# Rotary embedding of the first block: the exchanged halves come by SBUF transfers in place of a TensorE permutation matmul

## The chip, the cores and the metric
One NeuronCore of one Trainium2 chip runs the whole program. The metric is the device time of one execution in microseconds (us). The times of three executions of the kernel before stand below. All readings of a trace are of one profiled execution.

## What is computed
Two blocks, each with two layers, run over one sequence of 256 tokens with 1024 channels, in float32. Only the first block's projection and its rotary embedding matter here (cut from the reference):

```
def apply_rope(x, positions):
    half = HEAD_DIM // 2                     # HEAD_DIM = 64
    ...
    x1, x2 = xf[..., :half], xf[..., half:]
    return jnp.concatenate([x1 * cos - x2 * sin, x2 * cos + x1 * sin], axis=-1)

h = rms_norm(x, attn_pre_gain)
u = h @ w_in
(qa, ka, va, qb, kcb, vcb, ksb, vsb, kwb, vwb, g_nsa, g_a, g_b) = split(u)
qa, ka, qb_rot, ks, kw = apply_rope of qa, ka, qb, ksb, kwb
```

Attention over a window, over compressed and over selected keys follows, then an output projection, and a feed-forward network with a convolution. The second block has no rotary embedding.

## The kernel before
**Layout.** The projection `u` is held transposed: 128 channels (two heads of 64) on the partitions and 256 tokens along each. One such [128, 256] array is a tile of `U1`. In each of the two layers (`L`) of the first block there are 16 tiles, numbered t = 0 to 15. Eleven of them are rotated: `ROPE = [0, 1, 2, 3, 4, 6, 7, 8, 9, 12, 14]`, and their place in this list is r. Tiles 5, 13 and 15 are values (`VALS`), which are transposed; 10 and 11 are inputs of the compression.

**Weights.** Weights stream from HBM in chunks of about 1 MB, in a fixed order c0, c1, ... that is counted anew for each layer here: c0 to c7 are the eight panels of `w_in`, and panel x gives the tiles 2x and 2x+1. Then come c8 (branch gates), c9 (first compression weight), c10 (gates), c11 (second compression weight), c12 and c13 (gates), c14 (branch output). SyncE (SP) issues two transfers of 512 KB for each into one of three slots of `raw`; the load of chunk n waits until chunk n-3 has been split (`wlo_ready`, `load`). ScalarE (ACT) rounds a chunk to `whi` (L543), VectorE (DVE) subtracts to get `wlo` (L891): the two halves that give a float32 product out of rounded ones. Both run in a ring of four.

**A tile.** TensorE (PE) multiplies `whi` and `wlo` with the activations (L1452, L1455) into one of four banks of PSUM. ACT copies the low part out (`low`), DVE adds it (L899) into `U1`, which counts up `tile_out`. PE waits at tile t for the sum of tile t-4.

**The rotation of a tile (before).** PE multiplies the tile in float32 with `C("swap")`, a 128x128 permutation that exchanges partitions i and i^32 within each 64 (L1650), into bank 6 or 7. GpSimd (POOL) writes `cq` = tile x cos (L1355). DVE writes `tm` = bank x signed sin (L1038) and adds `cq` to it (L1041), in place in `U1` or, for tiles 6 to 9, into `QR`. `tm` and `cq` have two buffers each.

**Order.** Each engine runs its own list in program order. DVE's step c (0 to 11, the loop over `in_cs`) is: split a chunk (c+3), sum the tiles 2c and 2c+1, then `rope(r)` for the rotated ones among the tiles 2c-2 and 2c-1. In layer 0, while c is under 4, the split stands at the end of the step. In layer 0, step 2 also has `parameters()`, and step 3 the split of the gate weights. Steps 6 and 7 end with `cmp_build`, and steps 7 and 8 have `cmp_lo`, which feeds the compression. ACT's step c is: round chunk c+3, copy low parts, and, after a key tile (4, 12, 14), wait for its rotation and copy it with exchanged heads (`KSW`). PE's step c is: the two tiles of panel c, then the matmuls with `swap` of tiles 2c-2 and 2c-1, and the transposes of a value tile (L1662), which wait for its sum and, for tile 5 in layer 0, for `params_ready`. At c = 4 PE multiplies gate weights (L1627), at c = 5 it does four small products (L1633, L1634). At c = 8 the first gates' tiles are interleaved with the first compression (L1601), which waits for the sum of tile 14 and for `cmp_lo(0)`.

**SP's list.** For each layer it is c0, c1, ..., c6, then the two gain vectors broadcast into `G1` and `G2` (`gains`, L447 and L441, 512 KB written by each), then c7, c8 and so on.

Of the kernel before, what the change touches and what calls it, by code (L numbers as in the profile page):

```python
# [10 lines left out]
ALU = mybir.AluOpType  # L11
# [5 lines left out]
S = 256  # L17
# [22 lines left out]
Z_MAX = 20.0  # L40


CONST = {"ident": 128, "swap": 128, "ntri": 128, "stick": 128, "mask_a": 256, "mask_c": 256, "pair": 24,
         "mask_cmp": 32, "count": 32, "width": 2, "freq": 1, "sign": 1}
CONST_AT, _n = {}, 0
for _k, _w in CONST.items():
# [5 lines left out]
def host_constants():  # L52

    c = np.zeros((P, CONST_COLS), np.float32)

    def put(name, a):
        at, w = CONST_AT[name]
        c[:, at:at + w] = np.asarray(a, np.float32).reshape(P, w)
    i = np.arange(P)
    put("ident", np.eye(P))  # L60
    put("swap", (i[:, None] == (i ^ 32)[None, :]))
    put("ntri", np.where(i[:, None] >= i[None, :], -1.0, 0.0))
    put("stick", np.where(i[:, None] < i[None, :], 0.0, NEG))
    tri = np.where(i[None, :] <= i[:, None], 0.0, NEG)
    put("mask_a", np.concatenate([np.where(i[None, :] > i[:, None], 0.0, NEG), tri], 1))
    put("mask_c", np.concatenate([np.zeros((P, P)), tri], 1))
    put("pair", (i[:, None] % 24 == np.arange(24)[None, :]) & (i[:, None] < 48))
    end = np.arange(16) * 16 + 31
    end[15] = 1 << 20
    t = np.stack([i, i + P], 1)  # L70
    put("mask_cmp", np.where(end[None, None, :] <= t[:, :, None], 0.0, NEG))
    width = np.where(i[:, None] < 64, [[2, 8]], [[4, 16]])
    put("count", 1.0 / np.minimum(np.arange(1, 17)[None, None, :], width[:, :, None]))
    put("width", 1.0 / width)
    put("freq", np.float32(10000.0) ** (-(i % 32).astype(np.float32) / np.float32(32)))
    put("sign", np.where(i % 64 < 32, -1.0, 1.0))
    return c
# [90 lines left out]
def build(nc, a, out):  # L168
# [120 lines left out]
    wg_hi, wg_split, gates_part, gates_copied = sem("wg_hi"), sem("wg_split"), sem("gates_part"), sem("gates_copied")  # L289
    cur_ready, gain_ready = sem("cur_ready"), sem("gain_ready")  # L290
    gates_sum, gates_ready = sem("gates_sum"), sem("gates_ready")
    swap_ready, swap_used = sem("swap_ready"), sem("swap_used")
    cosmul_ready, rope_done, kswap_done = sem("cosmul_ready"), sem("rope_done"), sem("kswap_done")
    vt_ready, vt_out = sem("vt_ready"), sem("vt_out")
    cmp_in, cmp_hi, cmp_rhs, cmp_hid = sem("cmp_in"), sem("cmp_hi"), sem("cmp_rhs"), sem("cmp_hid")
# [128 lines left out]
    def _(sp):  # L424
# [26 lines left out]
        def panel(c, w_, c0):  # L451
# [2 lines left out]
            d = raw[:, c % RAW, :].rearrange("p (k n) -> p k n", n=256)  # L454
            load(c, [(d[:, x:x + 4], v[:, x:x + 4]) for x in (0, 4)])

        def two(c, views):

            d = raw[:, c % RAW, :].rearrange("p (m k n) -> p m k n", m=2, n=P)
            load(c, [(d[:, m], v_.rearrange("(k p) n -> p k n", p=P)) for m, v_ in enumerate(views)])  # L460
# [17 lines left out]
        sp.dma_start(const[:, 0:P], a["const"][:, 0:P]).then_inc(ident_in, 16)  # L478
        for L, p in enumerate(PLAN.one):
            n = 2 * L  # L480
            for s, (c, _) in enumerate(p["in"]):
                panel(c, a["w_in"][L], s * 256)
                if c == 0:
                    sp.dma_start(X[:, 1, :], a["x"][0, P:2 * P, :]).then_inc(x_in[1], 16)
                    sp.dma_start(posi[:, :], a["positions"][0:1, :].broadcast_to([P, S])).then_inc(consts_in, 16)
                    sp.dma_start(const[:, at:], a["const"][:, at:]).then_inc(consts_in, 16)
                if c == 1:
                    sp.dma_start(const[:, P:at], a["const"][:, P:at]).then_inc(masks_in, 16)
                if s == 6:
                    gains(n + 1)  # L490
            for j in range(EARLY):
                gate(L, j, p["early"][j][0])
                if j < 2:
                    c = p["cmp"][j][0]
                    v = a["cmp_w1"][L, j].rearrange("(k p) n -> p k n", p=P)
                    d = raw[:, c % RAW, :].rearrange("p (k n) -> p k n", n=P)
                    load(c, [(d[:, x:x + 8], v[:, x:x + 8]) for x in (0, 8)])
            for kind, x, c, _ in p["branch"]:
                if kind == "gate":
                    gate(L, x, c)  # L500
                else:
                    d = raw[:, c % RAW, :].rearrange("p (b k n) -> p b k n", b=2, n=256)
                    load(c, [(d[:, b], a[nm][L, :, x * 256:x * 256 + 256].rearrange("(k p) n -> p k n", p=P))
                             for b, nm in enumerate(("w_branch_a", "w_branch_b"))])
            token_major(p["out"], a["w_out"][L])
            for j, (c, _) in enumerate(p["up"]):
                two(c, [a["ffn_w_up"][L, :, j * P + b * FF:j * P + b * FF + P] for b in range(2)])
                if j == 6:
                    gains(n + 2)
            token_major(p["down"], a["ffn_w_down"][L])  # L510
# [368 lines left out]
    def _(dve):  # L879
# [149 lines left out]
        for L, p in enumerate(PLAN.one):  # L1029
# [3 lines left out]
            def rope(r):  # L1033

                t = ROPE[r]
                dst = U1[:, PLACE[t], :] if t < 6 or t > 9 else QR[:, t - 6, :]
                dve.wait_ge(swap_ready, 11 * L + r + 1)
                v.tensor_tensor(tm[:, r % 2, :], bank[6 + r % 2][:, 0:S], sinT[:, :], ALU.mult).then_inc(swap_used, 1)  # L1038
                dve.wait_ge(swap_used, 11 * L + r + 1)
                dve.wait_ge(cosmul_ready, 11 * L + r + 1)  # L1040
                v.tensor_tensor(dst, cq[:, r % 2, :], tm[:, r % 2, :], ALU.add).then_inc(rope_done, 1)  # L1041

            def cmp_build(n):

# [390 lines left out]
    def _(pe):  # L1435
# [150 lines left out]
        for L, p in enumerate(PLAN.one):  # L1586
# [28 lines left out]
            for c in range(9):  # L1615
# [26 lines left out]
                                                  rows[:, r, :], ident)  # L1642
                    ins.then_inc(rows_t, 1)
                for t in (2 * c - 2, 2 * c - 1):
                    if t in ROPE:
                        r = ROPE.index(t)
                        pe.wait_ge(tile_out, t0 + t + 1)
                        if r >= 2:
                            pe.wait_ge(swap_used, 11 * L + r - 1)
                        mm(bank[6 + r % 2][:, 0:S], C("swap"), U1[:, PLACE[t], :], start=True, stop=True, **g32)\  # L1650
                            .then_inc(swap_ready, 1)
                    if t in VALS:
                        n = VALS.index(t)
                        pe.wait_ge(tile_out, t0 + t + 1)
                        if n:
                            pe.wait_ge(vt_out, 3 * L + n)
                        elif L == 0:
                            pe.wait_ge(params_ready, 1)
                        else:
                            pe.wait_ge(tile_out, t0 + 6)  # L1660
                        for b in range(2):
                            ins = nc.tensor.transpose(bank[5][:, b * P:b * P + P], U1[:, PLACE[t], b * P:b * P + P], ident)  # L1662
                        ins.then_inc(vt_ready, 1)
# [3 lines left out]
            pe.wait_ge(cmp_hid, 2 * L + 2)  # L1667
            pe.wait_ge(vt_out, 3 * L + 3)
            pe.wait_ge(cur_ready, L + 1)
            pe.wait_ge(swap_used, 11 * L + len(ROPE))  # L1670
            mm(bank[6][:, 0:30], w2cur[:, :, :].rearrange("p r d -> p (r d)"), HC[:, 0, :], start=True, stop=True, **g32)
            for g in range(2):
                ins = mm(bank[6][0:N_CMP, P + HD * g:P + HD * g + HD], HC[:, 1, N_CMP * g:N_CMP * g + N_CMP], w2all[:, L, 1, :],
# [236 lines left out]
```

## Time and profile before

| | us |
|---|---|
| three executions | 1738.45, 1739.1 and 1739.48; median 1739.1 |
| the profiled execution, first to last instruction (its span) | 1735.3 |
| TensorE busy | 1704.5 (98%) |
| VectorE busy | 1216.0 (70%) |
| ScalarE busy | 1021.0 (59%) |
| GpSimd busy | 691.9 (40%) |
| bytes moved by the transfers | 306.73 MB, mean 177 GB/s |

The executions are 3.8 us longer than the span of the profiled one: that is what lies before the first and after the last instruction. Shares are averages over stages with different limits. The stage of the change lies at 28 to 82 us in layer 0 and at 419 to 468 us in layer 1. The granted clock of TensorE is at its full level in all slices of the page.

### The profile page before, as it was taken

The page shows a single profiled execution, that of the slowest core. Times are in us where ns is not written, and L with a number is a line of the kernel's source. Part 1 is how long each engine was busy: PE and PEld are TensorE (multiplying, and loading weights), DVE is VectorE, ACT ScalarE, POOL GpSimd, SP SyncE. Part 2 cuts the span into 40 slices and gives each one's busy share as a digit, 9 for nine tenths or more (in the row PEclk, how much of TensorE's full clock was granted, in tenths as well). Part 3 has the DMA queues.
Part 4 walks back from the last instruction along what each step waited for, and adds up shares of the span by engine and source line. Part 5 has one row for each costly group of instructions (what it writes and reads, how often), then busy time and mean ns, then how long its engine had stood idle before and what let it go on. Part 6 is the DMA issues. An engine that isn't in the chain of part 4 may idle for free.

```text
span 1735.3 us, 26430 instructions
## 1 busy us (share of the span) xinstructions
PE 1704.5 (98%) x9926; PEld 1453.6 (84%) x9926; DVE 1216.0 (70%) x1840; ACT 1021.0 (59%) x1928; POOL 691.9 (40%) x666
## 2 busy tenths in 40 slices
PE   8999999999999999999999999999999999999998
PEld 6867898888867888889888887888898889788887
DVE  7776799967766799957666656766476656566663
ACT  5587666655577666646555556555465545565542
POOL 4134346601034256604661050775057600507640
PEclk9999999999999999999999999999999999999999
DMA  9633666576524567576766553866576565348662
GB/s 267 179 98 113 175 197 177 177 241 175 148 80 122 170 197 192 179 234 172 193 182 222 181 168 98 232 185 204 180 202 187 182 230 194 122 123 223 188 208 73
DMA packets 412226, 306.73 MB, mean 177 GB/s; under 512 B 10083, under 2 KB 366901, under 8 KB 412098
## 3 DMA queue, kind: packets, MB, share of 16 engines
q1 hardware_dynamic: 411314, 304.31, 59.8%
q8 instruction: 79, 1.29, 0.3%
q0 software_dynamic: 784, 0.72, 0.2%
q14 instruction: 49, 0.40, 0.1%
HBM read 303.94 MB, written 1.05 MB: 176 GB/s over the span
## 4 chain that ended last, share of the span: by engine, by line
PE 76%; DVE 15%; ACT 4%; issue 3%; DMA 2%; SPq 0%; DVEq 0%; ACTq 0%
PE bank L1452 24%; PE bank L1455 12%; PE bank L1550 8%; PE bank L1552 8%; PE bank L1551 8%; DVE wlo L891 6%; DVE CB L1216 6%; PE bank L1503 3%; PE bank L1516 3%; PE bank L1513 3%; DVE UB L899 2%; DMA raw<-in_w_in 2%; ACT whi L543 1%; PE bank L1757 1%; ACT PB L546 1%
## 5 line engine op out<-in xcount | busy, mean ns | idle before, releaser
L891 DVE TENSOR_TENSOR wlo<-raw,whi 128x1024 fp32r<-128x1024 f32 (+1 forms) x568 | 734.8, 1319 | 176.2 <-ACT whi L543 172.8
L1452 PE MATMUL bank<-hsA,whi 128*128 128x512 f32 x2480 | 796.6, 398 | 0.6 <-DVE TA L899 0.6
L543 ACT ACTIVATE whi<-raw 128x1024 fp32r<-128x1024 f32 (+1 forms) x568 | 571.4, 1034 | 136.3 <-PE bank L1552 88.7
L1455 PEld LDWEIGHTS bank<-hsA,wlo 128*128 128x128 f32 x2480 | 466.2, 188 | 105.4
L1455 PE MATMUL bank<-hsA,wlo 128*128 128x256 f32 x2480 | 495.0, 279 | 0.0
L1452 PEld LDWEIGHTS bank<-hsA,whi 128*128 128x128 f32 x2480 | 384.1, 189 | 4.1 <-issue 3.3
L543 ACT ACTIVATE low<-bank 128x256 f32<-128x256 f32 (+1 forms) x404 | 150.2, 376 | 314.3 <-PE bank L1452 283.5
L1320 POOL TENSOR_TENSOR HB<-CB,UB 128x256 f32<-128x256 f32 x88 | 123.6, 1405 | 344.5 <-ACT CB L546 343.9
L1550 PE MATMUL bank<-whi,hid 128*128 128x512 f32 x528 | 206.1, 390 | 2.0 <-DVE wlo L891 2.0
L1552 PE MATMUL bank<-wlo,hid 128*128 128x512 f32 x528 | 205.5, 389 | 0.0
L1551 PE MATMUL bank<-whi,hid 128*128 128x512 f32 x528 | 205.4, 389 | 0.0
L899 DVE TENSOR_TENSOR UB<-bank,low 128x256 f32<-128x256 f32 x264 | 109.2, 416 | 114.9 <-ACT low L543 114.7
L1321 POOL TENSOR_TENSOR hid<-CB,UB 128x256 fp32r<-128x256 f32 x88 | 144.8, 1646 | 0.0
L1550 PEld LDWEIGHTS bank<-whi,hid 128*128 128x128 f32 x528 | 99.1, 188 | 22.9 <-DVE wlo L891 2.8
L1320 POOL TENSOR_TENSOR HB<-CB 128x256 f32<-128x256 f32 x44 | 61.9, 1408 | 140.6 <-ACT CB L546 140.6
L1552 PEld LDWEIGHTS bank<-wlo,hid 128*128 128x128 f32 x528 | 99.1, 188 | 20.6
L1551 PEld LDWEIGHTS bank<-whi,hid 128*128 128x128 f32 x528 | 99.1, 188 | 20.5
L1216 DVE SCALAR_TENSOR_TENSOR CB<-UB,convT,CB 128x256 f32<-128x256 f32 x176 | 114.0, 705 | 0.0
L1322 POOL TENSOR_TENSOR hid<-HB,hid 128x256 fp32r<-128x256 f32 x132 | 109.7, 831 | 10.4
L1516 PE MATMUL bank<-hsA,wlo 128*128 128x256 f32 x464 | 96.5, 284 | 3.1 <-ACT hsA L543 3.1
L1513 PE MATMUL bank<-hsA,whi 128*128 128x256 f32 x464 | 94.2, 283 | 0.0
L1516 PEld LDWEIGHTS bank<-hsA,wlo 128*128 128x128 f32 x464 | 78.8, 192 | 5.0 <-issue 5.0
(226 smaller groups left out, 1885.5 us busy)
## 6 DMA issues: line engine op xcount, KB each, us to landing
raw<-in_ffn_w_up SPq DMA_DIRECT2D x176, 512.0 KB, 5.2
raw<-in_ffn_w_down SPq DMA_DIRECT2D x120, 512.0 KB, 4.6
raw<-in_w_in SPq DMA_DIRECT2D x104, 512.0 KB, 5.9
raw<-in_ffn_w_gate SPq DMA_DIRECT2D x88, 512.0 KB, 4.0
raw<-in_w_out SPq DMA_DIRECT2D x32, 512.0 KB, 4.5
raw<-in_ffn_w_down SPq DMA_DIRECT2D x24, 256.0 KB, 3.0
G<-in_norm_g SPq DMA_DIRECT2D x12, 512.0 KB, 7.1
raw<-in_cmp_w SPq DMA_DIRECT2D x8, 512.0 KB, 5.0
```

Of the source, the lines that this page charges most:

```text
L543: return nc.scalar.activation(out_, in_, func, **kw)
L891: v.tensor_tensor(wlo[c_ % RING][:, x:y], raw[:, c_ % RAW, x:y], whi[c_ % RING][:, x:y].bitcast(F32), ALU.subtract)\
L1216: ins = v.scalar_tensor_tensor(y[:, n, :], UB[:, j % 2, n, k:S + k], convT[:, k, at:at + 1], y[:, n, :], ALU.mult, ALU.add)
L1320: g_.tensor_tensor(HB[:, j % 2, :], x, y, ALU.mult)
L1321: seq.link(g_.tensor_tensor(dst[:, 0:S], x, y, ALU.mult))
L1452: return mm(out_[:, 0:2 * n], whi[slot][:, at:at + P], rhs[:, 0:2 * n], start=x == 0, stop=False, **g32)
L1455: return mm(out_[:, n:2 * n], wlo[slot][:, at:at + P], rhs[:, 0:n], start=False, stop=False, **g32)
L1513: return mm(out_, whi[c % RING][:, at(m, k):at(m, k) + P], both(k, 1), start=False, stop=j == 0 and k == KD - 1, **g32)
L1516: return mm(tile_bank(t + m)[:, S:2 * S], wlo[c % RING][:, at(m, k):at(m, k) + P], hsA[:, k, 0:S], start=False, stop=j > 0 and k == KD - 1 ...
L1550: mm(y, hi, whi[s][:, x * HALF:x * HALF + HALF], start=k == k_first, stop=False, **g32)
L1551: mm(y, lo, whi[s][:, x * HALF:x * HALF + HALF], start=False, stop=False, **g32)
L1552: ins = mm(y, hi, wlo[s][:, x * HALF:x * HALF + HALF], start=False, stop=k == k_end, **g32)
```

## The change
The matmul with `swap` is gone, with its constant, its PSUM banks and PE's waits. SP now issues four transfers from SBUF to SBUF for each rotated tile. Each copies 32 partitions of the tile (32 KB) to the partitions of the other half, in the `tm` buffer of the tile. DVE multiplies that buffer in place with the signed sine. Before each group of four, SP waits for the tile's sum and for the end of the rotation two places before, which frees the buffer. The groups of panel x stand in SP's list right before the load of chunk x+7, in layer 0 for x under 4 right before that of chunk x+6. The constants are 128 columns narrower.

```
-                dve.wait_ge(swap_ready, 11 * L + r + 1)
-                v.tensor_tensor(tm[:, r % 2, :], bank[6 + r % 2][:, 0:S], sinT[:, :], ALU.mult).then_inc(swap_used, 1)
+                q = 11 * L + r
+                turned = tm[:, q % 2, :]
+                dve.wait_ge(swap_ready[q % 2], 64 * (q // 2) + 64)
+                v.tensor_tensor(turned, turned, sinT[:, :], ALU.mult).then_inc(swap_used, 1)
...
-                        pe.wait_ge(tile_out, t0 + t + 1)
-                        if r >= 2:
-                            pe.wait_ge(swap_used, 11 * L + r - 1)
-                        mm(bank[6 + r % 2][:, 0:S], C("swap"), U1[:, PLACE[t], :], start=True, stop=True, **g32)\
-                            .then_inc(swap_ready, 1)
...
+        def swap_rows(L, x):
+            for t in (2 * x, 2 * x + 1):
+                if t in ROPE:
+                    r = ROPE.index(t)
+                    q = 11 * L + r
+                    sp.wait_ge(tile_out, PLAN.one[L]["in"][0][1] + t + 1)
+                    if r >= 2:
+                        sp.wait_ge(rope_done, q - 1)
+                    for b in range(4):
+                        sp.dma_start(tm[32 * b:32 * b + 32, q % 2, :], U1[32 * (b ^ 1):32 * (b ^ 1) + 32, PLACE[t], :])\
+                            .then_inc(swap_ready[q % 2], 16)
...
+            behind = {first + x + (6 if L == 0 and x < 4 else 7): x for x in range(8)}
+            def turns_before(c):
+                if c in behind:
+                    swap_rows(L, behind[c])
             for s, (c, _) in enumerate(p["in"]):
+                turns_before(c)
                 panel(c, a["w_in"][L], s * 256)
```

`turns_before(c)` stands in the same way before the loads of the gates, of the compression weights and of the branch output.

## Rows read from the trace of the kernel before

**Rows 1.** The page: span, busy time of each engine, and the chain that ended last.
```profile
span 1735.3 us, 26430 instructions
...
PE 1704.5 (98%) x9926; PEld 1453.6 (84%) x9926; DVE 1216.0 (70%) x1840; ACT 1021.0 (59%) x1928; POOL 691.9 (40%) x666
...
PE 76%; DVE 15%; ACT 4%; issue 3%; DMA 2%; SPq 0%; DVEq 0%; ACTq 0%
```
**Rows 2.** Busy time by stretch: length, then PE, PEld, DVE, ACT, POOL, clock, DMA share, GB/s.
```profile
28.00:71.00 43.00, 42.80 (x243) 36.40 (x242) 38.10 (x65) 23.09 (x39) 13.48 (x17) 1.00 0.86 237
...
420.00:457.00 37.00, 36.50 (x202) 30.26 (x200) 30.04 (x51) 17.87 (x32) 7.68 (x9) 1.00 0.73 205
```
**Rows 3.** The instructions of L1650: duration min/median/max in ns, first and last start.
```profile
L1650 PE MATMUL bank<-U,const x44: 377/379/483, 28.0 to 466.1; 128*128 128x256 f32 x44
```
**Rows 4.** The chain in order of time, PE's part of L1650: start, us.
```profile
49.74 0.86 PE bank L1650 x4
```
**Rows 5.** TensorE in order of time: start, us, line, operation, [idle before].
```profile
41.94 0.38 PE L1662 MATMUL bank<-const,U 128*128 128x128 f32 x2
...
70.91 0.27 PE L1601 MATMUL bank<-RH,whi 128*128 128x60 f32 x1 [0.20 <-DVE U L899]
...
419.44 1.02 PE L1650 MATMUL bank<-U,const 128*128 128x256 f32 x4
420.64 1.46 PE L1650 MATMUL bank<-U,const 128*128 128x256 f32 x4 [0.18 <-DVE tm L1038]
427.53 0.59 PE L1650 MATMUL bank<-U,const 128*128 128x256 f32 x2
...
456.93 0.27 PE L1601 MATMUL bank<-RH,whi 128*128 128x60 f32 x1 [0.20 <-DVE U L899]
```
**Rows 6.** VectorE in order of time, layer 0.
```profile
31.24 0.41 DVE L1038 TENSOR_TENSOR tm<-bank,sinT 128x256 f32<-128x256 f32 x1
...
34.50 2.89 DVE L891 TENSOR_TENSOR wlo<-raw,whi 128x1024 fp32r<-128x1024 f32 x2
...
39.66 0.43 DVE L1041 TENSOR_TENSOR U<-cq,tm 128x256 f32<-128x256 f32 x1
...
64.60 0.42 DVE L899 TENSOR_TENSOR U<-bank,low 128x256 f32<-128x256 f32 x1 [2.14 <-ACT low L543]
```
**Rows 7.** VectorE in order of time, layer 1.
```profile
420.07 0.42 DVE L1038 TENSOR_TENSOR tm<-bank,sinT 128x256 f32<-128x256 f32 x1 [1.93 <-PE bank L1650]
...
433.53 2.36 DVE L891 TENSOR_TENSOR wlo<-raw,whi 128x1024 fp32r<-128x1024 f32 x2 [2.26 <-ACT whi L543]
```
**Rows 8.** ScalarE in order of time, layer 1: the key tile, then the next chunk.
```profile
431.31 0.84 ACT L543 ACTIVATE KSW<-U 64x256 f32<-64x256 f32 x2 [3.19 <-DVE U L1041]
```
**Rows 9.** Issues at 28 to 29 us: name, queue, count, KB, us from issue to landing.
```profile
raw<-in_w_in SPq DMA_DIRECT2D x1, 512.0 KB, 9.8
```
**Rows 10.** The same, issues at 414.6 to 415.2, then at 417 to 418 us.
```profile
G<-in_attn_post_gain SPq DMA_DIRECT2D x1, 512.0 KB, 9.4
...
raw<-in_w_in SPq DMA_DIRECT2D x1, 512.0 KB, 8.7
```
**Rows 11.** The same, small issues at 0 to 20 us.
```profile
const<-in_const SPq DMA_DIRECT2D x1, 34.0 KB, 8.0
...
rows<-in_pool_scale POOLq DMA_DIRECT2D x1, 2.0 KB, 2.1
```
**Rows 12.** SP's queue in order of time: start, us for the issue, line.
```profile
1.19 0.32 SPq L477 DMA_DIRECT2D gain<-in_attn_pre_gain  x1
...
4.01 0.87 SPq L486 DMA_DIRECT2D const<-in_const  x1
...
28.01 0.76 SPq L435 DMA_DIRECT2D raw<-in_w_in  x1
...
415.43 1.16 SPq L441 DMA_DIRECT2D G<-in_ffn_pre_gain  x1
...
76.83 0.37 SPq L435 DMA_DIRECT2D raw<-in_w_branch_a  x1
```

More of the change, by code:

```diff
@@ L40 @@
 Z_MAX = 20.0
-CONST = {"ident": 128, "swap": 128, "ntri": 128, "stick": 128, "mask_a": 256, "mask_c": 256, "pair": 24,
+CONST = {"ident": 128, "ntri": 128, "stick": 128, "mask_a": 256, "mask_c": 256, "pair": 24,
          "mask_cmp": 32, "count": 32, "width": 2, "freq": 1, "sign": 1}
@@ L60, in host_constants @@
     put("ident", np.eye(P))
-    put("swap", (i[:, None] == (i ^ 32)[None, :]))
     put("ntri", np.where(i[:, None] >= i[None, :], -1.0, 0.0))
@@ L291, in build @@
     gates_sum, gates_ready = sem("gates_sum"), sem("gates_ready")
-    swap_ready, swap_used = sem("swap_ready"), sem("swap_used")
+    swap_ready, swap_used = [sem("swap_ready0"), sem("swap_ready1")], sem("swap_used")
     cosmul_ready, rope_done, kswap_done = sem("cosmul_ready"), sem("rope_done"), sem("kswap_done")
@@ L480, in _ @@
             n = 2 * L
+            first = p["in"][0][0]
+            behind = {first + x + (6 if L == 0 and x < 4 else 7): x for x in range(8)}
+            def turns_before(c):
+                if c in behind:
+                    swap_rows(L, behind[c])
             for s, (c, _) in enumerate(p["in"]):
+                turns_before(c)
                 panel(c, a["w_in"][L], s * 256)
@@ L491, in _ @@
             for j in range(EARLY):
+                turns_before(p["early"][j][0])
                 gate(L, j, p["early"][j][0])
@@ L494, in _ @@
                     c = p["cmp"][j][0]
+                    turns_before(c)
                     v = a["cmp_w1"][L, j].rearrange("(k p) n -> p k n", p=P)
@@ L498, in _ @@
             for kind, x, c, _ in p["branch"]:
+                turns_before(c)
                 if kind == "gate":
@@ L1036, in rope @@
                 dst = U1[:, PLACE[t], :] if t < 6 or t > 9 else QR[:, t - 6, :]
-                dve.wait_ge(swap_ready, 11 * L + r + 1)
-                v.tensor_tensor(tm[:, r % 2, :], bank[6 + r % 2][:, 0:S], sinT[:, :], ALU.mult).then_inc(swap_used, 1)
+                q = 11 * L + r
+                turned = tm[:, q % 2, :]
+                dve.wait_ge(swap_ready[q % 2], 64 * (q // 2) + 64)
+                v.tensor_tensor(turned, turned, sinT[:, :], ALU.mult).then_inc(swap_used, 1)
                 dve.wait_ge(swap_used, 11 * L + r + 1)
                 dve.wait_ge(cosmul_ready, 11 * L + r + 1)
-                v.tensor_tensor(dst, cq[:, r % 2, :], tm[:, r % 2, :], ALU.add).then_inc(rope_done, 1)
+                v.tensor_tensor(dst, cq[:, r % 2, :], turned, ALU.add).then_inc(rope_done, 1)
             def cmp_build(n):
@@ L1644, in _ @@
                 for t in (2 * c - 2, 2 * c - 1):
-                    if t in ROPE:
-                        r = ROPE.index(t)
-                        pe.wait_ge(tile_out, t0 + t + 1)
-                        if r >= 2:
-                            pe.wait_ge(swap_used, 11 * L + r - 1)
-                        mm(bank[6 + r % 2][:, 0:S], C("swap"), U1[:, PLACE[t], :], start=True, stop=True, **g32)\
-                            .then_inc(swap_ready, 1)
                     if t in VALS:
@@ L1669, in _ @@
             pe.wait_ge(cur_ready, L + 1)
-            pe.wait_ge(swap_used, 11 * L + len(ROPE))
             mm(bank[6][:, 0:30], w2cur[:, :, :].rearrange("p r d -> p (r d)"), HC[:, 0, :], start=True, stop=True, **g32)
```

## The prediction

> **What bounds the kernel now.** I read the page first: TensorE is busy for 98% of the span and carries 76% of the chain that ended last [rows 1]. Taken alone that says that every matmul removed is time won. But shares are averages, so the next view is the busy time of the stretch in which the rotations lie. In layer 0, from 28 to 71 us, PE is busy for 42.80 of 43 us, and DVE for 38.10: DVE has only 4.9 us to spare in seven and a half steps. In layer 1, from 420 to 457, DVE has 37 - 30.04 = 7.0 us to spare [rows 2]. So PE binds, and DVE is close behind it, closest in layer 0. The same rows show the transfers at a share of 0.86 and 0.73.
>
> PE in order of time shows where the two meet: the first compression matmul, at 70.91 and at 456.93, waits for a DVE sum [rows 5]. Before it stands DVE's wait of 2.14 us for tile 13 at 64.60 [rows 6], then `cmp_build`, a split, `cmp_lo` and the sum of tile 14, some 6.3 us of DVE work without a gap. I call this point the meeting. Whatever moves the meeting moves everything behind it, and I work out its shift for each layer.
>
> **What is removed.** A rotated tile has two instructions on L1650, 44 in all for 22 tiles [rows 3]. Their 379 ns overlap; what they occupy is read from the chain: four take 0.86 us, so 0.43 us a tile [rows 4]. Nine tiles lie ahead of PE's last tiles before the meeting: 3.9 us in layer 0. In layer 1 the first four tiles cost more, since PE waits there for `tm` to free a bank: from 419.44 to about 421.8, 2.3 us (the second four start at 420.64 and end with a stall on their buffers) [rows 5]; with five more (2.2 us) 4.5 us. The eleventh tile comes behind the meeting, 0.43 us. If nothing else happened and DVE kept up, 22 x 0.43 = 9.5 us, and some more in layer 1, would be the gain.
>
> **What is added on DVE.** The multiplication reads `tm` and not PSUM. The two DVE operations of a rotation, one of which reads PSUM and one only SBUF, take 0.41 and 0.43 us where nothing disturbs them [rows 6], so I count no difference. Removing DVE's wait for PE (1.93 us in layer 1 [rows 7]) is worth something only if the rows are there sooner than the matmul was.
>
> **What is added on SP and the transfers.** There are 88 transfers of 32 KB. No row shows one from SBUF to SBUF. Two prices are needed.
> - *Issue.* The nearest rows are 0.32 us (4 KB) and 0.37 us (512 KB, quiet queue); while the queue is full the 34 KB constant took 0.87 and a gain 1.16 [rows 12]. I take 0.4 us, that of the quiet rows with a gap, so 1.6 us a tile and 3.2 us for a panel of two. The ends are 0.32 and 0.87.
> - *Landing.* The floor is the 2.1 us of a 2 KB transfer on a quiet queue. A small transfer behind loads lands late: the 34 KB constant took 8.0 us [rows 11]. I take it that a transfer lands no sooner than the load issued before it on SP's queue, and at least 2.1 us after its issue.
>
> The Trainium skill, in "DMA: Bandwidth & Descriptors", under "Anatomy of one DMA", gives a transfer a fixed cost of about 2.0 us and little more at this size; by that alone the rows would always be in time, and the sum would be that of rival B. The same page, under "Queues, rings and completion order", has each DMA engine consume descriptors in ring order, which speaks against this change: the rows stand behind whatever SP issued before. The constant's 8.0 us is on the side of the second, and no row shows a small SBUF transfer overtaking a load.
>
> **Layer 0, step by step.** SP's groups for panel 0 stand behind c5. The second half of c5 is issued at 28.01, taking 0.76, and lands 9.8 us later, at 37.8 [rows 9, 12]. The rows of tiles 0 and 1 are issued by 32.0 but land at about 38. DVE wanted them at 31.24 [rows 6]: it now stands still for nearly 7 us. Queued behind that wait on DVE are the rotations, the split of c4, the sums of tiles 4 and 5, and `parameters`. From 38.2: two rotations (1.7) to 39.9, the split (2.8, as the 2.89 at 34.50 [rows 6]) to 42.7, sums (0.7, two of 0.42 that overlap) to 43.4, parameters (1.2) to 44.6. PE has done panel 3 by 39.8 and needs tile 5's sum and the parameters for the transposes that ran at 41.94 [rows 5]: it waits until 44.6. The rows of panel 1 are issued after rotations 0 and 1, 39.1 to 42.3, behind the two gains; they land at about 45.8, so DVE waits another 1.2 us. From there DVE runs without a break: rotations to 47.6, split c5 50.0, sums and gate split 51.2, rotation 52.0, c6 54.4, c7 56.8, sums 57.5, rotations 59.2, c8 62.1, sums 62.8, rotations (the rows land behind c10, at 63.0) 64.7, c9 67.1, sums 67.8, `cmp_build` 70.4, c10 72.8, `cmp_lo` and sum 73.9. PE alone would get to the meeting at 72.0: 45.0 + four stretches of 5.56, 1.84, 5.56 and 1.3, 5.56 us = 65.2, and then the 6.8 us from the end of tile 13 to the meeting. So DVE ends last: 73.9 against 70.9 is +3.0, less 0.4 for the eleventh tile, +2.5. A shorter form of the same: 6.8 us of standing still, less the 4.9 that DVE had to spare, is +1.9, which is the low end.
>
> **Layer 1.** SP's groups for panel 0 stand behind the second gain and before c7. The first gain, issued at 414.72, lands 9.4 us later, at 424.1; c7's first half, issued at 417.51, lands 8.7 us later, at 426.2 [rows 10]. The rows land between them, at 425.3, where DVE had started at 420.07 [rows 7]. It stands still 5.2 us longer. Rotations to 427.0, split c5 to 429.9, sums of tiles 4 and 5 to 430.6. PE is at its transposes at 425.2 (427.53 less 2.3) and waits until 430.7: 2.8 us later than before, of which the four tiles still to be removed give back 1.7, so +1.0 at the meeting by PE. DVE's side has one more link: ACT waits for rotation 4 before it rounds c7 (it waited 3.19 us at 431.31 [rows 8], and DVE then 2.26 us for c7 [rows 7]). Rotation 4 now ends at 437.3, as its rows land behind c8, so `whi` of c7 is half ready at 439.6, and DVE goes on from there: c7 442.0, sums and rotations 444.4, c8 447.2, sums 447.9, rows behind c10 at 448.5, rotations 450.2, c9 and sums 453.3, `cmp_build` 455.9, c10 458.3, the rest 459.4: +2.5 against 456.93. The eleventh tile is behind the meeting and DVE, ACT and the next loads do not wait for PE there, so I give nothing for it. The low end is +1.0.
>
> **Sum.** 2.5 + 2.5 = +5.0 us on a profiled span of 1735.3, and the same on the median of 1739.1: 1744.1 us. By the low ends 1.9 - 0.4 + 1.0 = +2.5, 1741.6; with two or three later landings of a microsecond, 1748.
>
> **Rivals.**
> - *A, the forecast:* the first rows of each layer land behind queued loads, DVE stands still, and PE's gain is spent and more. 1744.1, from 1741.5 to 1748.
> - *B, the transfers are not held up by the queue* and land 2.1 us after issue: 32.5 and 34.0 in layer 0, where DVE multiplied at 31.24 [rows 6] and, for tile 1, 2 us later. DVE then is about 0.6 us late, loses its waits for PE and most of the 2.14 for tile 13, so the meeting moves by -1.9, and with the eleventh tile -2.3. In layer 1 the rows land at 420.3 and 421.9; the transposes then wait for the sums at 426.3 in place of 428.0, the four later tiles give 1.7, and the meeting moves by about -3.0. Together -5.3: 1733.8. For it: 32 KB is little. Against it: the 8.0 us of the constant.
> - *C, held up, but less:* parts of the queue are passed, and the first rows land 2 us sooner (36 and 423.3). Each microsecond there is one at the meeting, until DVE's spare time covers it: 5.0 - 4 = +1, 1740.
> - *D, SP becomes the bound:* each issue costs 0.87 us as in the full queue. A panel with two rotated tiles then takes 8 x 0.87 + 1.0 for a load = 8.0 us of SP, against the 6.2 that DVE takes a step; it decides from (6.2 - 1.0) / 8 = 0.65 us an issue. Panels 1, 3 and 4 have two tiles: the last rows come 1.4, 1.7 and 2 us too late, some 5 us a layer on top of A: 1754. For it: the issues of 0.87 and 1.16 lie in these full stretches. Against it: those had over 100 descriptors each.
>
> **How the numbers follow.** A 0.58, B 0.12, C 0.18, D 0.12. A measurement of this kernel can tell about 0.2% from no change, 3.5 us: 1735.6 to 1742.6. Faster is B, 0.12. The same is C and the low fifth of A, 0.30. Slower is the rest of A and D, 0.58. A's own range is 1741.5 to 1748; for 8 in 10 the range takes in C and part of D, and leaves out B and the top of D: 1736 to 1751.
>
> **What would show it.** In the trace after, DVE's first `tm` operation of each layer tells most: about 38 and 425.3 with a wait for a transfer of some 7 and 7 us is A; 32.5 and 420.3 is B. PE's transposes of tile 5 should wait for DVE, some 4 to 5 us in each layer. The first L1601 should start at about 73.9 in layer 0. DVE should be busy nearly without a gap from 46 to 74. SP's issues of `tm` should take 0.4 us each; 0.65 or more would be D. The forecast is wrong if small transfers pass the loads, or if DVE has more to spare than its order in program lets me count.

## The result

The changed kernel takes 1787.8 us (median of four; 1786.2 to 1788.7) against 1739.05 for the kernel before on the same chip: a ratio of 1.0283, 95% interval 1.0271 to 1.0295. It is 48.8 us slower, where 5 were forecast. The profiled execution has a span of 1786.9 us, 51.6 more than that of before [rows 1], and this difference is what is accounted for below.

The page of the changed kernel, the lines that answer to [rows 1], and the clock by slice:

```profile
span 1786.9 us, 26427 instructions
...
PE 1734.8 (97%) x9882; PEld 1480.7 (83%) x9882; DVE 1216.5 (68%) x1840; ACT 1022.4 (57%) x1928; POOL 691.7 (39%) x666
...
PEclk9869999999959999999999999999999999999999
...
PE 73%; DVE 16%; ACT 3%; DMA 3%; issue 3%; SPq 2%; DVEq 0%; ACTq 0%
```

TensorE has 44 instructions fewer and is busy for 30 us more. The line of clocks says why: slices 2, 3 and 12 (each is 44.7 us) show 8, 6 and 5 tenths of the full clock. VectorE's busy time has not changed. Busy time by stretch, with the columns of [rows 2] (length, PE, PEld, DVE, ACT, POOL, clock, share, GB/s):

```profile
44.00:51.00 7.00, 5.95 (x20) 5.17 (x21) 4.07 (x12) 1.45 (x3) 0.78 (x1) 0.51 0.85 256
51.00:78.00 27.00, 23.80 (x132) 19.33 (x130) 21.37 (x34) 12.91 (x22) 5.61 (x5) 1.00 0.74 185
79.00:119.00 40.00, 36.94 (x137) 33.50 (x138) 18.46 (x31) 14.65 (x26) 0.73 (x1) 0.50 0.46 128
...
457.00:464.00 7.00, 3.54 (x12) 3.08 (x13) 6.03 (x10) 0.00 (x0) 2.30 (x2) 0.51 0.39 83
491.00:532.00 41.00, 37.70 (x140) 34.25 (x141) 19.37 (x32) 14.93 (x27) 0.73 (x1) 0.50 0.48 125
```

The granted clock fell from 2.4 to 1.2 GHz four times, for 6.8, 41.0, 6.8 and 41.0 us by the trace's record, 96 us in all (the last microseconds of the program, where it falls in every kernel here, are left out). In the kernel before it was at its full level in every slice of the page. Each fall came while TensorE stood still. Its waits in the changed kernel (layer 0, then layer 1; what it waited for, us in total, times, longest):

```profile
PE bank L1626 <- DVE U L922: 5.3, 1, 5.3
PE bank L1680 <- DVE nsink L1048: 3.8, 1, 3.8
PE bank L1680 <- DVE U L922: 2.0, 1, 2.0
...
PE bank L1680 <- DVE U L922: 8.2, 1, 8.2
PE bank L1626 <- DVE U L922: 5.3, 1, 5.3
```

L1680 is the transpose of a value tile and L1626 the first compression matmul (L1662 and L1601 before). Three points of TensorE's list divide the 51.6 us: the meeting in each layer, and the transposes at the entry of layer 1. In the kernel before the last of these began here:

```profile
406.48 1.04 PE L1486 MATMUL bank<-const,H 128*128 128x128 f32 x8
```

and in the changed kernel, in order of time (start, us, [idle before]):

```profile
45.05 0.66 PE L1680 MATMUL bank<-const,U 128*128 128x128 f32 x2 [3.82 <-DVE nsink L1048]
...
82.06 0.39 PE L1626 MATMUL bank<-RH,whi 128*128 128x60 f32 x1 [5.30 <-DVE U L922]
...
433.51 1.04 PE L1511 MATMUL bank<-const,H 128*128 128x128 f32 x8
...
494.30 0.39 PE L1626 MATMUL bank<-RH,whi 128*128 128x60 f32 x1 [5.31 <-DVE U L922]
```

| stretch | before | changed | shift |
|---|---|---|---|
| start to the meeting of layer 0 | 70.9 [rows 5] | 82.1 | +11.2 |
| from there to the entry of layer 1 | 335.6 | 351.4 | +15.9 |
| from there to the meeting of layer 1 | 50.5 | 60.8 | +10.3 |
| from there to the end | 1278.4 | 1292.6 | +14.2 |

So 21.5 us are lost ahead of the meetings, where 5 were forecast, and 30.1 us behind them, where of the change only the rotation of tile 14 lies. Behind each meeting stand the 41 us at half clock.

What holds VectorE, in order of time, the lines that answer to [rows 6] and [rows 7]:

```profile
38.22 0.42 DVE L1063 TENSOR_TENSOR tm<-tm,sinT 128x256 f32<-128x256 f32 x1 [5.43 <-DMA tm<-U]
...
47.67 0.42 DVE L1063 TENSOR_TENSOR tm<-tm,sinT 128x256 f32<-128x256 f32 x1 [2.77 <-DMA tm<-U]
...
70.88 0.43 DVE L1063 TENSOR_TENSOR tm<-tm,sinT 128x256 f32<-128x256 f32 x1 [5.02 <-DMA tm<-U]
...
454.77 0.42 DVE L1063 TENSOR_TENSOR tm<-tm,sinT 128x256 f32<-128x256 f32 x1 [9.59 <-DMA tm<-U]
```

And SP's queue, first its issues in order of time, then the line of the new transfers (ns min/median/max):

```profile
29.71 6.70 SPq L466 DMA_DIRECT2D tm<-U  x8
...
61.09 3.50 SPq L434 DMA_DIRECT2D raw<-in_w_in  x2
64.69 6.10 SPq L466 DMA_DIRECT2D tm<-U  x8
...
L466 SPq DMA_DIRECT2D tm<-U x88: 507/592/2162, 29.7 to 497.5; - x88
```

The first rows of layer 0 land at 38.2, as forecast. But eight issues take 6.1 to 6.7 us and not 3.2, and at panel 4 SP begins them only at 64.7, behind the load of c10, when VectorE is about to want them.

### The profile page after: what moved, and what is told of

Read it like the earlier page. It is cut to its first block, busy times and chain, and to the rows that moved or that the text cites. A ratio compares the mean times of both kernels' runs of the same rounds, so it can differ in the third digit from the quotient of the medians.

```text
span 1786.9 us, 26427 instructions
## 1 busy us (share of the span) xinstructions
PE 1734.8 (97%) x9882; PEld 1480.7 (83%) x9882; DVE 1216.5 (68%) x1840; ACT 1022.4 (57%) x1928; POOL 691.7 (39%) x666
## 4 chain that ended last, share of the span: by engine, by line
PE 73%; DVE 16%; ACT 3%; DMA 3%; issue 3%; SPq 2%; DVEq 0%; ACTq 0%
PE bank L1477 23%; PE bank L1480 12%; PE bank L1575 8%; PE bank L1577 8%; PE bank L1576 8%; DVE wlo L914 7%; DVE CB L1241 6%; PE bank L1528 3%; PE bank L1541 2%; PE bank L1538 2%; DVE UB L922 2%; DMA tm<-U 2%; SPq L466 1%; DMA raw<-in_w_in 1%; ACT whi L566 1%
## 5 line engine op out<-in xcount | busy, mean ns | idle before, releaser
L1477 PE MATMUL bank<-hsA,whi 128*128 128x512 f32 x2480 | 818.2, 407 | 0.6 <-DVE TA L922 0.6
L1480 PEld LDWEIGHTS bank<-hsA,wlo 128*128 128x128 f32 x2480 | 478.6, 193 | 106.6
L1480 PE MATMUL bank<-hsA,wlo 128*128 128x256 f32 x2480 | 508.7, 285 | 0.0
L1477 PEld LDWEIGHTS bank<-hsA,whi 128*128 128x128 f32 x2480 | 396.0, 194 | 4.4 <-issue 3.6
L1347 POOL TENSOR_TENSOR hid<-HB,hid 128x256 fp32r<-128x256 f32 x132 | 109.6, 831 | 10.3
L1541 PE MATMUL bank<-hsA,wlo 128*128 128x256 f32 x464 | 96.5, 284 | 3.1 <-ACT hsA L566 3.1
L1541 PEld LDWEIGHTS bank<-hsA,wlo 128*128 128x128 f32 x464 | 78.8, 192 | 5.0 <-issue 5.0
```

Source lines behind the costliest of these rows:

```text
L1477: return mm(out_[:, 0:2 * n], whi[slot][:, at:at + P], rhs[:, 0:2 * n], start=x == 0, stop=False, **g32)
L1480: return mm(out_[:, n:2 * n], wlo[slot][:, at:at + P], rhs[:, 0:n], start=False, stop=False, **g32)
L1541: return mm(tile_bank(t + m)[:, S:2 * S], wlo[c % RING][:, at(m, k):at(m, k) + P], hsA[:, k, 0:S], start=False, stop=j > 0 and k == KD - 1 ...
```

## The experiments

After the result there were two theories. K: TensorE's stalls bring the half clock, and the half clock is most of the loss. W: the waits and the slower transfers are the loss, and the clock is beside the point. Of what makes the stalls, L says that it is the landing behind queued loads, and I that it is SP's issues. Each run was timed beside the kernel before, whose median was 1736.9 to 1738.2 us in these rounds; a difference "to before" is to that median. Traces are of one execution each.

**The clock, in the changed kernel.** Matmuls that nobody reads fill TensorE's stalls (float32, some 0.43 us each).

```
+            def keep(n):
+                for _ in range(n):
+                    mm(bank[7][:, 0:S], ident, C("mask_a"), start=True, stop=True, **g32)
...
+                    keep((12, 12)[L])          # ahead of the first compression matmul
+                        if n == 0: keep((9, 19)[L])          # ahead of tile 5's transposes
+                        if n == 1 and L == 0: keep(4)        # ahead of tile 13's transposes
```

> The changed kernel, with float32 matmuls whose result nobody reads put on TensorE ahead of the waits where it stood still for VectorE (9 and 19 before the transposes of tile 5 in layers 0 and 1, 4 before those of tile 13 in layer 0, 12 before the first compression in each layer; about 0.43 us each at the full clock). Nothing that VectorE, SP or the transfers do is changed. Theory K (the granted clock): most of the 49 us is TensorE work at half the clock, which begins when it stands still; with TensorE kept at work the clock stays at its full level, only the delay of the meeting remains, some 6 to 11 us a layer, and the time is 1752 to 1762. Rival W (the waits themselves and the slower transfers are the loss): the time stays at 1787 or rises by what the added matmuls overshoot, whatever the clock does.

1761.2 us, ratio 1.0135 (1.012 to 1.015): 24.1 us above before, where the changed kernel is 48.8 above. So some 25 us came back by adding work. From 79 to 119 us the same stretch now reads

```profile
79.00:119.00 40.00, 38.37 (x262) 33.33 (x261) 29.82 (x71) 22.35 (x49) 1.01 (x2) 1.00 0.69 190
```

with 262 matmuls in place of 137. The three points of TensorE's list are here

```profile
84.16 0.27 PE L1631 MATMUL bank<-RH,whi 128*128 128x60 f32 x1 [0.16 <-DVE U L922]
...
420.23 1.03 PE L1511 MATMUL bank<-const,H 128*128 128x128 f32 x8
...
480.17 0.27 PE L1631 MATMUL bank<-RH,whi 128*128 128x60 f32 x1
```

so the meetings come no earlier, and behind them the kernel runs as fast as before: 336.1 and 1277.7 us for 335.6 and 1278.4, where the changed kernel took 351.4 and 1292.6. So K holds, at the upper end of what was expected: the 30.1 us behind the meetings, half of the loss or more, are the clock. The transfers of the changed kernel are all still there. The clock still fell once for 3.4 us.

**A stall alone, without any transfer.** The kernel before, with a chain of multiplications put on VectorE. In `held` 18 of them (8.3 us) stand ahead of the first rotation; in `held_meet` 7 (3.2 us) right ahead of the meeting; `held_meet_warm` is `held_meet` with 7 unread matmuls on TensorE ahead of the first compression matmul. Nothing is moved by transfers in these three.

```
+                if r == 0:                                  # held; held_meet: if c == 7, range(7), before the tile sums
+                    for _ in range(18):
+                        seq.link(v.tensor_tensor(tm[:, L, :], sinT[:, :], sinT[:, :], ALU.mult))
...
+                    for _ in range(7):                      # held_meet_warm, at c == 8
+                        mm(bank[4][:, 0:S], ident, C("mask_a"), start=True, stop=True, **g32)
```

> The kernel before (permutation by matmul, no transfers), with 18 multiplications on VectorE, each waiting for the one before, about 0.46 us each and 8.3 us together, ahead of the first rotation of each layer; their result is overwritten. It puts a stall of the size of the one seen into VectorE alone. Theory K: TensorE stands still for some 5 us in each layer ahead of tile 5's transposes, and again at the meeting if VectorE is still behind; if either brings the half clock, the time is 1750 to 1775; the direct delay without the clock is 2 x (8.3 - 5 to 7 of spare time), 1742 to 1746. Rival W: 1742 to 1746 whatever the clock does.

> The kernel before, with 7 linked multiplications on VectorE (3.2 us) in each layer ahead of the sums of tiles 14 and 15, that is right before the meeting of TensorE and VectorE; their result is overwritten. Theory P (where TensorE stands still decides how long the clock stays low: behind the meeting come the compression's small matmuls, and it stayed at half for 20 to 41 us there, against 7 to 10 us behind a stall of 5 to 6 us ahead of panel 3 or 4): TensorE waits 3.2 us at its first compression matmul, the clock falls to half for 13 to 41 us in each layer, and the time is 1755 to 1772. Rival W (a stall costs its own length): 2 x 3.2, 1744 to 1747.

> The same as held_meet, with 7 float32 matmuls whose result nobody reads on TensorE ahead of the first compression matmul, 3.0 us, the length of the stall. VectorE's delay is the same. Theory P: the clock stays at its full level and the time is that of a stall alone, 1744 to 1747; the difference to held_meet is then the price of the clock after one stall of 3 us. Rival W: both are the same.

| kernel | us | to before, us | half clock in the trace, us |
|---|---|---|---|
| held | 1753.3 | +16.2 | 6.8 and 10.2 |
| held_meet | 1759.7 | +21.5 | 17.1 and 20.5 |
| held_meet_warm | 1745.35 | +7.2 | 3.4 |

By the three points of TensorE's list, in the traces, in us against the kernel before ("to" is the stretch that ends at a meeting, "behind" the one after it):

| kernel | to, layer 0 | behind | to, layer 1 | behind |
|---|---|---|---|---|
| changed | +11.2 | +15.9 | +10.3 | +14.2 |
| warm | +13.3 | +0.5 | +9.5 | -0.7 |
| held | +8.0 | +0.4 | +8.7 | -0.7 |
| held_meet | +2.9 | +8.7 | +3.2 | +7.8 |
| held_meet_warm | +4.1 | 0.0 | +3.2 | +1.2 |

The three times lie where K and P (the same theory, for the meeting) put them, and those of `held` and `held_meet` above the ranges of W. Only the kernels with 17 us or more at half clock behind a meeting lose more than about 1 us there.

The last two are the clearest pair of the study. VectorE is held for the same time. The first line is TensorE's wait in `held_meet`, the same in each layer; then the same stretch behind the meeting of layer 0 in `held_meet`, and in the fence below it in `held_meet_warm`:

```profile
PE bank L1604 <- DVE U L899: 3.4, 1, 3.4
...
74.00:95.00 21.00, 21.00 (x92) 18.95 (x92) 9.67 (x20) 8.37 (x15) 0.53 (x1) 0.59 0.25 76
```

```profile
74.00:95.00 21.00, 20.62 (x142) 18.68 (x141) 14.31 (x27) 12.49 (x22) 0.74 (x1) 1.00 0.46 130
```

Two stalls of 3.4 us cost 7.2 us if TensorE is kept at work through them, and 21.5 us if it is not. The clock's price is 14.4 us for 34.2 us more at half (37.6 less 3.4), 0.42 us for each. In the changed kernel it is 30.1 us for the 82 us behind the meetings, 0.37 for each. And the place counts: `held` makes longer waits on TensorE (5.3 and 6.4 us, before the swap matmul) in the middle of the projection, the clock is back after 7 to 10 us, and nothing is lost behind the meetings; a wait of 3.4 us at the meeting is followed by 17 to 20 us at half, where the first gates' tiles are interleaved with the compression's matmuls of 60 and 30 columns. What in that stretch keeps the clock down was not tested, nor why it stays down for 41 us in the changed kernel and for 20 here.

The spare time of VectorE that the prediction counted, 4.9 us in layer 0 and 7.0 in layer 1, did not show: a hold of 8.3 us in `held` moved the meetings by 8.0 and 8.7 us. How much of that is the half clock ahead of them (6.8 and 10.2 us) was not separated.

The Trainium skill, in "TensorE: Matmul & The Clock Gate", Part 1, says that a monitor of TensorE's activity gates its clock between 1.2 and 2.4 GHz. The traces agree with the levels: the granted share is 1.00 or 0.50. The Trainium skill, on the same page under "Terms", prices the slow time (`throttle_active_nc0_time_ns`) at that time x (1 - K/N), here a half. The 0.37 and 0.42 measured are less; why was not tested.

**The transfers with nobody waiting.** The kernel before, with the 88 issues at their places, from a constant to an unused array.

```
+                        sp.dma_start(ang[32 * b:32 * b + 32, 4 + q % 2, :], C("mask_a")[32 * (b ^ 1):32 * (b ^ 1) + 32, :])
```

> The kernel before (permutation by matmul), with the 88 transfers of 32 rows issued by SP at the places they have in the changed kernel, from a constant array to an array that nobody reads; the rotation does not wait for them. It shows what the issues and the bytes cost when nobody waits. Theories K and I: the loads of weights have time to spare, so 1738 to 1743. Rival C (the transfers slow the loads and through them everything): 1750 or more, with ScalarE waiting longer for weights.

1751.4 us, 14.3 above before, ratio 1.0091 (1.0066 to 1.0117). This missed: I had expected no change. Three of the four executions took 1750.9 to 1751.8 us; the traced one is the fourth, 1760.2, so what is read from its trace is larger than in the others. Nobody waits for these rows, yet SP is busy with them (507 to 2969 ns each, median 591), and the weights behind them come late. ScalarE's waits at 20 to 82 us, to be held against 7.7 us for weights in the kernel before, all of it for `in_w_in`:

```profile
ACT whi L571 <- DMA raw<-in_w_in: 14.2, 6, 5.3
...
ACT whi L571 <- DMA raw<-in_cmp_w: 4.3, 1, 4.3
```

TensorE then waited 3.6 us at the meeting of layer 0 and 1.1 in layer 1, and the clock was at half for 20.5 and 13.7 us behind them, and later for 3.4 more. So the transfers alone, issues and bytes together, are a second cause, and in this trace they are paid mostly through the clock.

**Fewer issues.** `one_transfer` has one transfer of 128 rows a tile, unexchanged; `quarter` has only the first of the four, so a quarter of the rotation's rows are moved.

```
-                    for b in range(4):
+                    for b in range(1):                      # quarter
...
+                    sp.dma_start(tm[:, q % 2, :], U1[:, PLACE[t], :]).then_inc(swap_ready[q % 2], 16)   # one_transfer
```

> The changed kernel with one transfer of 128 rows for each rotated tile in place of four of 32 rows: the same bytes, a quarter of the issues. The rows arrive in their old order, so the two halves of each head are not exchanged. Theory I (the issues on SP, about 0.8 us each, are what makes the rows of the later panels late): SP's part of a panel falls from 6.4 to about 1.6 us, VectorE's waits from panel 1 on disappear, the first wait of each layer stays (the rows still land behind queued loads, at 38 us), and the time is 1744 to 1758, the upper part if the clock still falls after the first stall. Rival L (landing behind loads is all of it): the waits of the later panels stay as long as they are, and the time stays at 1780 or more.

> The changed kernel with one of the four transfers of each rotated tile (rows 32 to 63 to rows 0 to 31; the other three parts of the array hold what was in them, so the rotation is not computed for them). Size and form of a transfer are those of the changed kernel, only their number is a quarter: 1.6 us of SP for a panel of two tiles in place of 6.4. Theory I+L (the first wait is the landing behind c5, all later ones are SP's issues): VectorE waits some 5 us at its first rotation in each layer, and less than 1 us together at the later ones before the meeting; TensorE stands still 2 to 4 us before tile 5's transposes and under 1 us at the meeting, which comes at about 73 in layer 0; if that little keeps the clock up behind the meeting, the time is 1742 to 1752, with 7 us at half in each layer. If later waits for transfers of 5 us remain, the number of issues is not their cause, and the time is above 1765.

1775.3 and 1774.1 us, 38.2 and 36.5 above before; their executions spread by 8 to 11 us, and neither theory's range holds them. The meeting of layer 0 comes at 75.8 and 76.3 in place of 82.1, with a quarter of the issues in both and with all of the bytes in the one. VectorE's waits in `quarter` are the first landing, as long as ever, and little behind it:

```profile
38.00 0.43 DVE L1065 TENSOR_TENSOR tm<-tm,sinT 128x256 f32<-128x256 f32 x1 [5.96 <-DMA tm<-U]
...
45.80 0.42 DVE L1065 TENSOR_TENSOR tm<-tm,sinT 128x256 f32<-128x256 f32 x1 [1.11 <-DMA tm<-U]
...
65.46 0.43 DVE L1065 TENSOR_TENSOR tm<-tm,sinT 128x256 f32<-128x256 f32 x1 [1.71 <-DMA tm<-U]
```

In layer 1 the stretch from the entry to the meeting is shorter by 5.0 and 5.6 us. So the number of issues is worth 5 to 6 us at each meeting, and I was right on that; but I had expected the clock to survive what is left, and it did not: in `quarter` TensorE waits 2.7 and 2.2 us at the meetings, in `one_transfer` 2.5 and 2.0, and it stays at half for 34 us behind each. In `quarter` it is busy for 34.00 of the 34 us from 77 to 111, and the clock does not come back in them. That is why the time falls by only 11 to 12 us: of the 37.0 us that the trace of `quarter` is longer than before, 26.8 lie behind the meetings. `one_warm` was to take the clock out of this comparison:

> The changed kernel with one transfer of 128 rows a rotated tile (rows in their old order, so the halves are not exchanged), and with matmuls that nobody reads on TensorE ahead of its waits (7 and 13 before the transposes of tile 5, 5 and 4 before the first compression). With the clock held in both, the difference to the run warm (1761.2) is what four issues a tile cost over one. Theory I (the issues cost as much as the landing): 1745 to 1752. Rival L (only the first landing in each layer counts): 1758 to 1762.

1769.7 us, from 1761.2 to 1776.4, in neither range. The filling was too short: TensorE still waited 1.8 us at the meeting of layer 0 and ran at half for 34 us. It says nothing on the issues, but it shows that even 1.8 us of waiting there can be followed by the half clock. In its layer 1 a wait of 2.8 us at the meeting was not: the clock fell only 30 us later, for 6.8 us.

**The landing of the first rows.** `panel0_matmul` exchanges tiles 0 and 1 by the matmul again; `rows_earlier` puts the group of panel 0 one chunk earlier; `pool_queue` has GpSimd issue all groups.

```
+    return r > 1                                            # panel0_matmul: those with transfers
...
+            behind = {first + x + (6 if L == 0 and x < 4 else 7) - (x == 0): x for x in range(8)}   # rows_earlier
...
+                for b in range(4):                          # pool_queue, ahead of the product with the cosine
+                    pool.dma_start(tm[32 * b:32 * b + 32, q % 2, :], U1[32 * (b ^ 1):32 * (b ^ 1) + 32, PLACE[t], :])
```

> The changed kernel with the tiles of panel 0 (r = 0 and 1) exchanged by the matmul again in both layers, the other nine by the four transfers. Theory L (the first landing behind queued loads starts the loss): VectorE has no wait of 5 us at its first rotation, TensorE does not stand still before the transposes of tile 5 or only for 1 to 2 us, and the meeting comes 4 to 6 us earlier in each layer; as long as a stall is left at the meeting the clock still falls there, so 1755 to 1775, and 1745 to 1752 if it does not fall. Theory I (SP's issues of 0.8 us set the pace of every panel): the stalls only move to the later panels, and the time is 1775 or more.

> The changed kernel with the group of panel 0 one chunk earlier in SP's list (before c5 in layer 0 and before c6 in layer 1), so one megabyte less stands ahead of it in the queue, and in layer 1 the two gains behind it. Theory L: the first rows land at about 33 to 35 us in place of 38 in layer 0 and 5 to 7 us earlier in layer 1; the meeting comes 2 to 4 us earlier in each layer, 1770 to 1782. Theory I: c5, c6 and what follows are issued 6 us later, the gain is lost in the next panels, 1785 or more.

> The changed kernel, with the four transfers of a rotated tile issued by GpSimd on its own queue, right before its product with the cosine, in place of SP. SP's list is that of the kernel before. Theory Q (the rows are late because they stand behind weights in SP's queue and because SP spends 0.8 us on each): they land within some 5 us of the tile's sum even in the full stretch (16 KB transfers on this queue landed in 5.2 us), VectorE's first wait shrinks from 5.4 to 1 to 4 us, and loads are on time; with four issues of about 1 us each before a product of 0.74, GpSimd may be the next bound in panels with two tiles. 1734 to 1750 if the clock holds. Rival C (the 16 engines are full, whatever the queue): the first rows still land at 36 to 38 us, and the time is above 1760.

1779.4, 1786.8 and 1788.9 us, 42.5, 49.9 and 50.8 above before: the first two in the ranges of I, the third in that of C. VectorE's waits, in three fences in this order:

```profile
46.11 0.42 DVE L1088 TENSOR_TENSOR tm<-tm,sinT 128x256 f32<-128x256 f32 x1 [6.90 <-DMA tm<-U]
...
69.65 0.43 DVE L1088 TENSOR_TENSOR tm<-tm,sinT 128x256 f32<-128x256 f32 x1 [5.44 <-DMA tm<-U]
```

```profile
32.72 0.80 DVE L1063 TENSOR_TENSOR tm<-tm,sinT 128x256 f32<-128x256 f32 x1 [1.30 <-DMA tm<-U]
...
48.00 0.42 DVE L1063 TENSOR_TENSOR tm<-tm,sinT 128x256 f32<-128x256 f32 x1 [7.80 <-DMA tm<-U]
```

```profile
38.99 0.43 DVE L1064 TENSOR_TENSOR tm<-tm,sinT 128x256 f32<-128x256 f32 x1 [7.79 <-DMA tm<-U]
```

Without transfers for panel 0 the first wait is simply that of panel 1, 6.9 us, and the meeting comes at 80.5, 1.5 us earlier. In layer 1 it helps more: the first wait is 4.0 us in place of 9.6, and the way from the entry to the meeting is 6.3 us shorter. With the rows a chunk earlier the first wait falls from 5.4 to 1.3 us, and the next rises from 2.8 to 7.8; in layer 1 it is 9.6 to 0.7 and 0.9 to 10.1. Either way, in layer 0 the full stretch of transfers, from 25 to 48 us, is met once, and panel 4 waits over 5 us as ever. GpSimd's queue did not help in that stretch either: it issued tile 0's rows from 31.1 to 33.2 us and they landed at 39.0. That speaks against the order within SP's queue as the only cause, and for the DMA engines being full; it does not separate the two in the changed kernel.

**Only where the transfers are quiet.** Tiles 12 and 14 by transfers, the other nine by the matmul (`return r > 8` in place of `r > 1`).

> The kernel before, with only tiles 12 and 14 (r = 9 and 10, panels 6 and 7) exchanged by four transfers each, at their places in the changed kernel's list, where the transfers are at about half load. SP has four issues a panel there, 3.2 us in a step of 6 to 7, and VectorE comes to the rotation a full step later. Theories L and I: no stall, TensorE saves 0.43 us a tile, of which that of tile 14 in layer 0 counts and that of tile 12 is lost at the meeting, where VectorE is last: 1737.5 to 1740, not to be told from before. Rival: any stall at the meeting brings the half clock, 1745 or more.

1736.95 us (eleven executions) against 1736.89, ratio 0.9996 (0.9987 to 1.0005): no difference that can be measured, a little under the 1737.5 to 1740 of theories L and I. The meeting is at 70.7, 0.2 us earlier, with a wait of TensorE of 0.6 us:

```profile
70.70 0.27 PE L1651 MATMUL bank<-RH,whi 128*128 128x60 f32 x1 [0.62 <-DVE U L944]
```

The rows are in time there, with four issues a panel. But the matmul ahead of the meeting gives TensorE nothing, since VectorE is last. No version that was run beats the kernel before.

## Why the prediction was wrong

Point by point, by its own steps:

- *What bounds the kernel:* right. VectorE is last at the meeting in every kernel run without added matmuls on TensorE.
- *What is removed, and VectorE's part:* right in size. TensorE lost 44 instructions, and the multiplication takes 0.42 us with its input in SBUF.
- *The first landing:* right in its time in layer 0, 38.2 us for about 38 forecast, with a wait of 5.4 us and not nearly 7, and TensorE's stall before tile 5's transposes ended at 45.05 for 44.6. The reason given, the order in SP's queue, is not shown: issued on GpSimd's queue the rows landed no sooner, at 39.0. In layer 1 VectorE waited 9.6 us for about 7 forecast. The fixed cost of about 2.0 us that the prediction took from the Trainium skill, "DMA: Bandwidth & Descriptors", is given there, in "Anatomy of one DMA", for a transfer issued by GpSimd. On SP's queue the 88 transfers took 1.8 to 8.3 us from issue to landing, 3.3 in the median.
- *The price of an issue:* mis-sized. 0.4 us was taken from rows of a quiet queue; the runs show a minimum of 0.51, a median of 0.59, and 6.1 to 6.7 us for eight in the full stretch, 0.8 each. The prediction had put its turning point at 0.65 and given the other side 0.12. With it stands the wait at panel 4: 5.0 us where I had 0.2. `quarter` and `one_transfer` put this term at 5 to 6 us a meeting.
- *The cost of the transfers to the weights:* left out. `spare_rows` shows +14 us with nobody waiting.
- *The meeting's shift:* +11.2 and +10.3 for +3.0 and +2.5 forecast. The mechanism was that of rivals A and D together, and larger: D's 1754 us was some 15 us, and 21.5 were lost ahead of the meetings. Whether the half clock of 6.8 us that follows the stall before tile 5 in each layer has a part in it is not shown: `warm`, with the clock up in layer 1 and nearly so in layer 0, has +13.3 and +9.5, though its filling may add some of that. One sum ahead of the meeting is off, without effect: TensorE's stretches from 45.0 add up to 64.8 and not 65.2.
- *The step that failed:* the sum ended at the meeting, with "whatever moves the meeting moves everything behind it". That took the rest to run at the speed of before. The page showed the full clock in all slices, and I read it as a property of the kernel, though the same sum forecast that TensorE would stand still for some 5 us before tile 5's transposes in each layer and for 1.9 us (73.9 less 72.0) at the meeting of layer 0. No rival had a stall that changes the speed of what follows. That is worth 30.1 of the 51.6 us by the table, and it is shown, and not only argued, by `warm`, where these 30.1 us are gone, and by the pair of `held_meet` (14.4 us for two stalls of 3.4 us).

Still open is how the 21.5 us ahead of the meetings divide between landing, issues, late weights and the first half-clock stretches: the parts act on each other, and the run meant to separate them with the clock held did not hold it.

## What to carry to other kernels

Before pricing a new wait, look at whether TensorE will stand still for it, and what TensorE runs behind: in a kernel that is at full clock throughout, a stall of 3 us can cost three times its length (21.5 us for two of 3.4), and whether it does depends on where it falls. Take the price of issuing many small transfers from rows of the stretch where they will be issued, and count them on the issuing queue against the weights behind them. Work taken off the critical engine gains nothing if the next engine is made to wait longer than it can spare, and spare time read from busy time may not be there: a hold of 8.3 us moved the meetings by 8.0 and 8.7.

## What the runs showed of the hardware

- The granted clock, after a wait of TensorE of 1.8 to 5.8 us ahead of the compression, stayed at 1.2 GHz for 17 to 41 us in the runs where it fell there. After waits of 3.3 to 8.6 us in the middle of the projection it was back after 3.4 to 10.2 us.
- It does not always fall: after waits of 0.6 us (`late_rows_only`) and of 2.8 us (layer 1 of `one_warm`) at the same place the clock stayed up, and after one of 1.1 us in `spare_rows` it was at half for 13.7 us.
- A transfer of 32 rows of 1 KB from SBUF to SBUF takes SP 0.51 to 2.2 us to issue, more than one of 512 KB from HBM on a quiet queue (0.37 [rows 12]). Issued by GpSimd, four take 2.0 us. From issue to landing it is 3.3 us in the median on SP's queue and 4.8 on GpSimd's.
- Filling TensorE's waits with matmuls that nobody reads made the changed kernel 1.4% faster (ratios 1.0135 and 1.0283 to before), without any change to its transfers.
